# A decoder block in one launch: F0 from 10 to 8, two of w_down's sums in place, seven raw slots in the down projection

## The reference, cut to what matters

```python
x = x + concat([o_diff, o_nsa]) @ w_out            # 512 x 1024
h = rms_norm(x, norm2)
x = x + (silu(h @ w_gate) * (h @ w_up)) @ w_down   # w_gate, w_up 1024 x 2816, w_down 2816 x 1024
return rms_norm(x, final_norm)
```

## Time and profile before

| | us |
|---|---|
| median of 3 runs | 660.74 (659.76 to 660.91) |
| the profiled execution, its own time | 660.69 |
| its span, first to last instruction | 658.9 |
| PE busy in the span | 646.3 (98%) |
| DVE, ACT, POOL busy | 452.1, 348.5, 265.2 |
| plain stage from tile 1's up on | 329.99 to 425.66 |
| mixed stage | 425.66 to 545.87 |
| down stage, to the last matmul | 545.87 to about 652.4 |

### The profile page before, as it was taken

One profiled execution on the slowest core, in us unless ns is written; L12 is line 12 of the kernel. 1 busy time (PEld: TensorE's weight loads), 2 busy tenths in 40 slices (PEclk: granted clock), 3 DMA queues, 4 the chain that ended last, 5 costly groups with the idle time before them and its releaser, 6 DMA issues.

```text
span 658.9 us, 11055 instructions
## 1 busy us (share of the span) xinstructions
PE 646.3 (98%) x3915; PEld 570.2 (87%) x3915; DVE 452.1 (69%) x929; ACT 348.5 (53%) x689; POOL 265.2 (40%) x158
## 2 busy tenths in 40 slices
PE   8999999999999999999999999999999999999996
PEld 7988988888899887888877888899999998888884
DVE  5434437745655777634489987469888797788894
ACT  7546446778654568615332362344444445655663
POOL 4766343585242440224466767343443320000222
PEclk9999999999999999999999999999999999999999
DMA  8989969469894982144699999887677858766553
GB/s 247 268 179 243 284 187 216 112 193 367 228 267 113 246 168 65 45 159 118 160 298 300 289 282 283 209 253 213 188 225 208 256 176 274 261 189 201 183 171 127
DMA packets 114774, 139.22 MB, mean 211 GB/s; under 512 B 5044, under 2 KB 74784, under 8 KB 114720
## 3 DMA queue, kind: packets, MB, share of 16 engines
q1 hardware_dynamic: 97880, 107.35, 51.4%
q0 software_dynamic: 14176, 26.64, 22.6%
q10 hardware_dynamic: 2664, 4.53, 2.0%
HBM read 132.19 MB, written 54.81 MB: 284 GB/s over the span
## 4 chain that ended last, share of the span: by engine, by line
PE 81%; issue 8%; POOL 7%; DVE 2%; ACT 1%; DMA 1%; POOLq 0%; DVEq 0%; ACTq 0%
PE bank L776 8%; PE bank L778 8%; PE bank L777 8%; PE bank L795 7%; PE bank L797 7%; PE bank L796 7%; PE bank L1107 6%; PE bank L1105 6%; PE bank L1106 6%; PE bank L948 6%; POOL w_lo L728 4%; PE bank L924 3%; PE bank L908 2%; PE bank L909 2%; POOL down_sums L746 1%
## 5 line engine op out<-in xcount | busy, mean ns | idle before, releaser
L728 POOL TENSOR_TENSOR w_lo<-raw,w_hi 128x1024 fp32r<-128x1024 f32 (+1 forms) x76 | 191.1, 2518 | 261.9 <-ACT w_hi L1148 261.2
L1148 ACT CAST w_hi<-raw 128x1024 fp32r<-128x1024 f32 (+1 forms) x141 | 144.3, 1028 | 151.6 <-PE bank L1107 43.8
L795 PE MATMUL bank<-xT_hi,w_hi 128*128 128x512 f32 x272 | 108.8, 400 | 1.7 <-POOL w_lo L728 1.4
L797 PE MATMUL bank<-xT_hi,w_lo 128*128 128x512 f32 x272 | 107.0, 393 | 0.0
L796 PE MATMUL bank<-xT_lo,w_hi 128*128 128x512 f32 x272 | 106.8, 393 | 0.0
L1774 DVE TENSOR_TENSOR w_lo<-raw,w_hi 128x1024 fp32r<-128x1024 f32 x66 | 79.4, 1204 | 33.3 <-ACT w_hi L1148 33.3
L1617 DVE CUSTOM_DVE_ANT_0 bank<-bank,bias 128x128 f32<-128x128 f32 (+3 forms) x96 | 47.6, 497 | 78.0 <-PE bank L909 42.1
L795 PEld LDWEIGHTS bank<-xT_hi,w_hi 128*128 128x128 f32 x272 | 51.2, 188 | 13.1 <-POOL w_lo L728 1.7
L797 PEld LDWEIGHTS bank<-xT_hi,w_lo 128*128 128x128 f32 x272 | 51.1, 188 | 11.7
L796 PEld LDWEIGHTS bank<-xT_lo,w_hi 128*128 128x128 f32 x272 | 51.3, 188 | 9.9 <-issue 0.2
L1229 ACT ACTIVATE E<-bank,nmax 128x128 f32<-128x128 f32 (+3 forms) x80 | 42.5, 532 | 32.5 <-DVE nmax L1617 31.6
(11 more groups left out here) (280 smaller groups left out, 1609.3 us busy)
## 6 DMA issues: line engine op xcount, KB each, us to landing
raw<-mixed_sums SPq DMA_DIRECT2D x24, 512.0 KB, 4.6
raw<-in_w_gate_dram SPq DMA_DIRECT2D x22, 512.0 KB, 6.5
raw<-in_w_in_dram SPq DMA_DIRECT2D x20, 512.0 KB, 5.9
down_sums<-in_w_down_dram SPq DMA_DIRECT2D x20, 512.0 KB, 10.4
raw<-down_sums SPq DMA_DIRECT2D x20, 512.0 KB, 4.3
raw<-in_w_up_dram SPq DMA_DIRECT2D x16, 512.0 KB, 5.3
raw<-in_w_down_dram SPq DMA_DIRECT2D x15, 512.0 KB, 3.5
mixed_sums<-in_w_up_dram SPq DMA_DIRECT2D x12, 512.0 KB, 12.1
```

The source lines that it names most:

```text
L728: nc.gpsimd.tensor_tensor(wv_lo(k)[:, 0:n], raw[:, k % RAW_SLOTS, 0:n], wv_hi(k)[:, 0:n].bitcast(F32), ALU.subtract).then_inc(s_split, 1)
L795: nc.tensor.matmul(bank[:, :], hi, xT_hi[:, kt, :], start=kt == 0, stop=False)
L797: return nc.tensor.matmul(bank[:, :], lo, xT_hi[:, kt, :], start=False, stop=kt == KT - 1)
L1148: nc.scalar.copy(wv_hi(k)[:, 0:n], raw[:, k % RAW_SLOTS, 0:n]).then_inc(s_whi, 1)
```

## The change

F0 becomes 8, so tiles 8 and 9 are a seventh mixed pair. `mixed_sums` covers 14 tiles and takes 28 sums: for the last two tiles one block of two tiles and four steps. The order of RING is turned so that the first unit takes a bank of gate tiles. The plain stage has 16 chunks; SP makes copies beside 12 of them (every fourth has none) and four in the mixed stage, 40 in all.

In the down stage the products come in another order: A11, S3 (T3), S1 (T1), S2 (T2), A12, S4, A22 (T4). `down_sums` has two places instead of four. T3 and T1 are copied and added as before. T2 = T3 + a quarter is made by adding the quarter into T3's place, group by group, once S3's load of that group has landed in SBUF; T4 in T2's place in the same way after S2's loads. So POOL's loop runs to the last chunk, 12 copies go, and 52 accumulating DMAs are issued instead of 48. Only product 3 is in RUNNING, and it goes to three quarters of the output.

Down chunks use seven raw slots: the three of before and four of `raw_more`, which lies where `xa` (the left halves of units 0 and 1) was, so SP waits for unit 1 of the last pair before it loads there. The order in which quarters of x come back (`BACK`) and in which the output is normed (`NORMED`) follows the new order of products.

The core of the diff:

```diff
@@ -113,20 +114,21 @@
-PRODUCTS = [(A11, ("w", 0, 0), 0), (S1, ("sum", T1), 1), (S2, ("sum", T2), 0), (A12, ("w", 1, 0), 2),
-            (S3, ("sum", T3), 0), (S4, ("w", 1, 1), 1), (A22, ("sum", T4), 0)]
+PRODUCTS = [(A11, ("w", 0, 0), 0), (S3, ("sum", T3), 1), (S1, ("sum", T1), 0), (S2, ("sum", T2), 2),
+            (A12, ("w", 1, 0), 0), (S4, ("w", 1, 1), 1), (A22, ("sum", T4), 0)]
-RUNNING = (2, 4)
-QUARTERS = [[(0, 0, 1)], [(1, 1, 1), (0, 1, 1)], [(0, 1, -1)], [(0, 0, 1)], [(1, 1, -1), (1, 0, 1)], [(0, 1, 1)], [(1, 0, 1)]]
+RUNNING = (3,)
+QUARTERS = [[(0, 0, 1)], [(1, 1, -1), (1, 0, 1)], [(1, 1, 1), (0, 1, 1)], [(0, 1, -1), (1, 1, -1), (1, 0, 1)], [(0, 0, 1)],
+            [(0, 1, 1)], [(1, 0, 1)]]
-F0 = 10
+F0 = 8
 SUMS = [(T3, (0, 1), ("w", 1, 1)), (T1, (0, 1), ("w", 0, 0)), (T2, (0, 0), ("sum", T3)), (T4, (1, 0), ("sum", T2))]
-WIDE = 4
-
-BACK = {(0, 5): (0, 0), (1, 1): (0, 1), (1, 3): (1, 1), (2, 1): (1, 0)}
+OF_DOWN = [(T3, (0, 1), ("w", 1, 1)), (T1, (0, 1), ("w", 0, 0)), (T2, T3, ("w", 0, 0)), (T4, T2, ("w", 1, 0))]
+PLACE = {T3: 0, T2: 0, T4: 0, T1: 1}
+
+BLOCKS = [(0, 4, 0, 2), (0, 4, 2, 2), (4, 4, 0, 2), (4, 4, 2, 2), (8, 4, 0, 2), (8, 4, 2, 2), (12, 2, 0, 4)]
+
+BACK = {(0, 5): (0, 0), (1, 1): (1, 1), (1, 3): (1, 0), (2, 1): (0, 1)}
-    for wides in ((0, 1), (2,)):
+    for blocks in ((0, 1, 2, 3), (4, 5, 6)):
         for to, begin, add in SUMS:
-            todo += [("mixed", to, (w_, kp), begin, add) for w_ in wides for kp in range(2)]
-    for to, begin, add in SUMS:
+            todo += [("mixed", to, (b,), begin, add) for b in blocks]
+    for to, begin, add in OF_DOWN:
         todo += [("down", to, (g,), begin, add) for g in range(GROUPS_M)]
     return todo
+    mixed0, down_from = n_fill + 2 * F0, n_fill + 2 * F0 + N_UNIT * N_PAIR
     copy_at = [6 + i for i in range(10)] + [27 + i // 2 for i in range(14)]
-    copy_at += [n_fill + i for i in range(20)] + [n_fill + 2 * F0 + 4 + 10 * i for i in range(4)]
-    add_at = copy_at[0:16] + [31] * 8 + copy_at[24:]
+    copy_at += [n_fill + i for i in range(16) if i % 4 != 3] + [mixed0 + 4 + 10 * i for i in range(4)]
+    in_place = [down_from + GROUPS_M + 3 + i for i in range(6)] + [down_from + 3 * GROUPS_M + 3 + 2 * i for i in range(6)]
+    add_at = copy_at[0:16] + [31] * 8 + copy_at[24:] + in_place
+    assert len(add_at) == len(todo)
+        with ExitStack() as more_raw:
+
+            raw_more = sb("raw_more", [P, MORE_SLOTS, 1024], F32, more_raw)
-        RING = [ps[0], ps[6], ps[3], ps[4], ps[5], ps[2], ps[7], ps[1]]
+        RING = [ps[6], ps[3], ps[4], ps[5], ps[2], ps[0], ps[7], ps[1]]
...
-        NORMED = [(0, 0), (1, 0), (2, 1), (3, 1), (0, 1), (1, 1), (2, 0), (3, 0)]
+        NORMED = [(2, 1), (3, 1), (0, 0), (1, 0), (0, 1), (1, 1), (2, 0), (3, 0)]
...
-                return sums[what[1], m0:m1, :, :].rearrange("k p n -> p k n")
+                return sums[PLACE[what[1]], m0:m1, :, :].rearrange("k p n -> p k n")
...
+        def slot_of(k):
+
+            d = (k - down0) % (RAW_SLOTS + MORE_SLOTS)
+            return d if k >= down0 and d >= RAW_SLOTS else ((down0 + d) if k >= down0 else k) % RAW_SLOTS
+
+        def raw_at(k):
+            n = slot_of(k)
+            return raw_more[:, n - RAW_SLOTS, :] if n >= RAW_SLOTS else raw[:, n, :]
...
-                if k >= RAW_SLOTS:
-                    low_done(sp, k - RAW_SLOTS)
-                dst = raw[:, k % RAW_SLOTS, :]
-                signal = s_raw[k % RAW_SLOTS]
+                held = [m for m in range(k) if slot_of(m) == slot_of(k)]
+                if held:
+                    low_done(sp, held[-1])
+                elif slot_of(k) >= RAW_SLOTS:
+                    sp.wait_ge(s_chunk, late(("mixed", (N_PAIR - 1, 1))))
+                dst = raw_at(k)
+                signal = s_raw[slot_of(k)]
...
-                kind, to, at_, _, add = todo[i]
-                pool.wait_ge(s_copied[i % 4], 16 * (i // 4 + 1))
+                kind, to, at_, begin, add = todo[i]
+                if i < len(copy_at):
+                    pool.wait_ge(s_copied[i % 4], 16 * (i // 4 + 1))
+                else:
+                    raw_landed(pool, index[("down", ([x_[1] for x_ in PRODUCTS].index(("sum", begin)), at_[0]))])
...
-            for k in range(down0):
+            for k in range(len(chunks)):
```

More of the change, by code:

```diff
@@ L53 @@
 RAW_SLOTS = 3
+MORE_SLOTS = 4
 SPLIT_SLOTS = 4
@@ L444, in hymba_block @@
         s_final_g = sem("s_final_g")
-        s_raw = [sem(f"s_raw{i}") for i in range(RAW_SLOTS)]
+        s_raw = [sem(f"s_raw{i}") for i in range(RAW_SLOTS + MORE_SLOTS)]
         s_bias = [sem(f"s_bias{i}") for i in range(BIAS_SLOTS)]
@@ L516, in hymba_block @@
         run = up_n
-        sums = nc.dram_tensor("down_sums", (len(SUMS), FP, P, 512), F32).ap()
+        sums = nc.dram_tensor("down_sums", (2, FP, P, 512), F32).ap()
         down0 = index[("down", (0, 0))]
-        NORMED = [(0, 0), (1, 0), (2, 1), (3, 1), (0, 1), (1, 1), (2, 0), (3, 0)]
+        NORMED = [(2, 1), (3, 1), (0, 0), (1, 0), (0, 1), (1, 1), (2, 0), (3, 0)]
         adds = [(n, rows_, dh, u) for n in range(N_PROD) for rows_, dh, _ in QUARTERS[n] for u in range(2)]
@@ L568, in sum_part @@
                 return part(what, at_[0])
-            return mixed_part(what, F0 + WIDE * at_[0], WIDE, 2 * at_[1], 2)
+            f0, n, k0, n_k = BLOCKS[at_[0]]
+            return mixed_part(what, F0 + f0, n, k0, n_k)
         def sum_done(eng, kind, to, at_):
@@ L663, in _ @@
                     if UNITS[j][1][0] == "sum":
-                        for kp in range(2):
-                            sum_done(sp, "mixed", UNITS[j][1][1], (2 * p_ // WIDE, kp))
+                        for b, (f0, n, _, _) in enumerate(BLOCKS):
+                            if f0 <= 2 * p_ < f0 + n:
+                                sum_done(sp, "mixed", UNITS[j][1][1], (b,))
                     sp.dma_start(dst[:, 0:1024].rearrange("p (k n) -> p k n", k=4),
@@ L673, in _ @@
                     sp.dma_start(dst[:, 0:chunk_cols(k)].rearrange("p (k n) -> p k n", k=src.shape[1]), src).then_inc(signal, 16)
-                for i in [i for i in range(len(todo)) if copy_at[i] == k]:
+                for i in [i for i in range(len(copy_at)) if copy_at[i] == k]:
                     _, to, _, begin, _ = todo[i]
@@ L708, in raw_landed @@
         def raw_landed(eng, k):
-            loads = sum(2 if chunks[m][0] == "vg" else 1 for m in range(k % RAW_SLOTS, k + 1, RAW_SLOTS))
-            eng.wait_ge(s_raw[k % RAW_SLOTS], 16 * loads)
+            loads = sum(2 if chunks[m][0] == "vg" else 1 for m in range(k + 1) if slot_of(m) == slot_of(k))
+            eng.wait_ge(s_raw[slot_of(k)], 16 * loads)
         @block.gpsimd
@@ L727, in split @@
                 high_done(pool, k)
-                nc.gpsimd.tensor_tensor(wv_lo(k)[:, 0:n], raw[:, k % RAW_SLOTS, 0:n],
+                nc.gpsimd.tensor_tensor(wv_lo(k)[:, 0:n], raw_at(k)[:, 0:n],
                                         wv_hi(k)[:, 0:n].bitcast(F32), ALU.subtract).then_inc(s_split, 1)
@@ L1147, in weights_hi @@
                     act.wait_ge(s_chunk, late(chunks[was]))
-                nc.scalar.copy(wv_hi(k)[:, 0:n], raw[:, k % RAW_SLOTS, 0:n]).then_inc(s_whi, 1)
+                nc.scalar.copy(wv_hi(k)[:, 0:n], raw_at(k)[:, 0:n]).then_inc(s_whi, 1)
             def square(src, junk, col, n):
@@ L1773, in split_down @@
                 n = chunk_cols(k)
-                nc.vector.tensor_tensor(wv_lo(k)[:, 0:n], raw[:, k % RAW_SLOTS, 0:n],
+                nc.vector.tensor_tensor(wv_lo(k)[:, 0:n], raw_at(k)[:, 0:n],
                                         wv_hi(k)[:, 0:n].bitcast(F32), ALU.subtract).then_inc(s_dlo, 1)
```

## The result

The changed kernel takes **664.25 us** (median of 7 runs, 662.76 to 666.16) where the kernel before takes 660.81 in the same job; ratio 1.0054, 95% interval 1.0036 to 1.0072. That is 3.4 us slower; 658.2 was forecast, and the range ended at 660.8.

What follows compares the result with a forecast made beforehand. PE, busy 646.3 of 658.9 us, was taken to bound the kernel. The terms gave 660.69 - 2.07 - 1.39 + 0.90 = 658.13 us, from the median 658.2, with a range of 656.8 to 660.8.

Steps and rivals of the forecast that it cites:

- Part 1: Tiles 8 and 9 become a mixed pair: PE time falls from 22.10 to 20.04 us, 2.07 us saved.
- Part 2: Plain stage: fewer copies let loads land earlier, so PE's two w_lo pauses go; 1.39 us saved, bounds 0 and 1.39.
- Part 3: Crossing to the mixed stage, two tiles earlier: DVE's backlog makes unit 4's w_lo late; 0.9 us lost, bounds 0 and 2.4.
- DVE's list: Crossing: DVE's work from 399.42 through unit 4's split, 12.15 us, ending at 411.6 with 2.0 us to spare.
- the 5.65: Crossing: us for up 7 and the seven short operations behind it, taken from the old kernel, already holding one POOL collision.
- Part 4: RING's order, the seventh pair's sums and the moved copies: no cost, hidden by PE.
- Part 5: Down stage: same 462 matmuls, 106.53 us; the new slots, DVE's longer run and the sums in place cost zero.
- Seven raw slots only load earlier: Down stage: the added raw slots bring loads forward and cost nothing, as ACT and DVE already keep up.
- The rival of sums one after another: Down stage: accumulations wait for each other, 8.6 us each; PE stands 8.4 us, 666.6 us; chance 0.05.
- The eight additions: Down stage, product 3's turn on DVE: eight where the longest run was six, 1.24 us more, still 1.5 us early; no cost.
- The sum: Whole kernel: 660.69 - 2.07 - 1.39 + 0.90 = 658.13 us, from the median 658.2.

Runs made afterwards that it cites:

- before_early_81: Kernel before, with two of chunk 31's eight additions put behind POOL's subtraction of chunk 32, and that held until 81 exps are done; 660.49 us, ratio 1.0013.
- split_83: Changed kernel, with POOL waiting before its subtraction of chunk 32 until ACT has done 83 exps; 663.11 us, ratio 1.0043.
- no_adds: Changed kernel without the twelve accumulations of T2 and T4 (products take T3's sums instead), and SP not waiting for them; 658.83 us, ratio 0.9977.
- three_slots: Changed kernel with only the three earlier raw slots in the down stage (MORE_SLOTS 0 instead of 4); 676.16 us, ratio 1.0244.
- back_late: Changed kernel with SP's four loads of x moved behind later chunks, the first from (0, 5) to (1, 3); 658.96 us, ratio 0.9981.
- sp_stands: Changed kernel with the four x loads behind later chunks, but SP still waiting at chunk (0, 5) until the last mixed unit ends; 661.60 us, ratio 1.0015.

## Why the prediction was wrong

**Part 1** right: 22.10 to 20.04 us, 2.06. The estimate from the Trainium skill (TensorE: Matmul & The Clock Gate, Back-to-back issue gap), 2.37, was 0.3 too high.

**Part 2** right: 1.4 us taken, 1.4 measured. Both pauses are gone. POOL's fourth and fifth subtractions of the stage, the two that PE had waited for, in the kernel after:

```profile
346.31 2.82 POOL L754 TENSOR_TENSOR w_lo<-raw,w_hi 128x1024 fp32r<-128x1024 f32 x1
349.70 2.40 POOL L754 TENSOR_TENSOR w_lo<-raw,w_hi 128x1024 fp32r<-128x1024 f32 x1 [0.58 <-ACT w_hi L1177]
```

They end at 349.13 and 352.10; before they ended at 353.14 and 359.24, just ahead of the starts in the earlier trace rows. Two things changed at once in the kernel after, the copies and the start of the stage. In before_early_81, with every copy in its place, the subtractions end at 352.96 and 358.37, and a start 0.59 us later is enough to lose both pauses. But split_83, where the stage starts at 329.90, no later than before, has no pause either: its two subtractions end at 348.36 and 351.85. So the earlier loads are enough by themselves. Taking the copies alone out of the kernel before wasn't tried.

**Part 3** mis-sized: 0.9 taken, 0 measured. The mixed stage is seven times 20.04. Of DVE's list, the two products took 2.9 us where about 0.8 was put (a collision), and the seven short operations hold one collision, as the 5.65 had it: so the list has the one extra collision that was to make unit 4 0.2 us late. But it begins 2.5 us earlier than I put it (first line, against 399.42 in the earlier trace rows), and unit 4's split (second line) ends at 411.45, 2.8 us before PE wants it at 402.80 + 4 x 2.862 = 414.25.

```profile
396.92 0.68 DVE L1885 TENSOR_TENSOR gate_n<-bank,sq 128x512 f32<-128x512 f32 x1
...
410.23 1.22 DVE L1803 TENSOR_TENSOR w_lo<-raw,w_hi 128x1024 fp32r<-128x1024 f32 x1
```

**Part 4, "Nothing", failed**: a change in when a batch of accumulations ends moved the subtraction behind it on POOL's queue. I had asked what a moved copy does to PE, not what is queued behind it on POOL. It costs 0.6 to 0.8 us, shown in the traces from both sides (0.76 back in split_83, 0.59 lost in before_early_81), and between 0.3 and 1.7 in the other runs. The Trainium skill (SBUF — State Buffer, Who interferes with whom) has the exclusive lock that fits it; I used it for 128x512 additions and not for a 128x8 product. In these traces the time was set by POOL's instruction and not by the size of DVE's. In no_adds and three_slots the product is recorded 0.44 and 0.24 us ahead of the subtraction and still ends with it, after 3.31 and 3.11 us; which of the two was really first can't be read from these traces.

**Part 5, "Zero" and "Seven raw slots only load earlier", is the step that failed**, 4.8 of the 5.5 us lost. The rival of sums one after another had the right stage and the wrong mechanism: the first pause is at 569.43, product 1, not at 3 or 6 where a load waits for its sum. Two errors make it up.
- I took the landing from the rows' median over a quiet stage, 4.6 us, for a stage to which I added accumulations. The row of the loaded stage had 11.7. And the engines' time says that they would be full: twelve accumulations (ten of 512 and two of 256 KB) at 2.86 us for 512 KB are 31 us in the stage's first 55. Of these 55 the loads already took some 39 us in the kernel before (a share of 0.84, 0.74, 0.62 and 0.63 in four stretches of 15 us): 70 us do not go into 55. That shows that loads will be late, not that PE waits: back_late has the same transfers, and there the loads begin early enough.
- "Seven raw slots only load earlier" is not so: I didn't read SP's order against the new schedule. The load of x that waits for the last mixed unit was there before too, but SP came to it when it was free. With seven slots SP comes to it 6 us early and stands, so product 1's first load is issued 0.66 us behind the stage's start and not 5.88 ahead of it, as in back_late. Each alone is free (no_adds, back_late); together they cost 4.8 us.

The eight additions were fine: in no_adds and back_late DVE has the same eight and PE doesn't pause. The fourth pause after, 0.4 us with the slower start behind it, ahead of 618.37, ends with the split behind them (618.32), but counted from the stage's start less the three pauses DVE begins that run 64.9 us in, 1.2 us later than in back_late (63.7): its loads had been late.

**The sum** with measured terms: 660.7 - 2.06 - 1.4 + 0 + 0.67 + 4.8 = 662.7, the profiled 662.76. The median lies 1.5 us above this execution; for that no cause is shown beyond what split_83's trace suggests (a longer pause in the down stage, and the slower clock behind it).

## What to carry to other kernels

Cost an added DMA by the time that it takes the DMA engines, and take the landing of its neighbours from a stage that is already so loaded. When a queue gets more to do, look in its order for instructions that wait: a stand that costs nothing while the DMA engines have time to spare (no_adds) is paid when they are full, and more slots can bring the queue to it early. And a batch that ends earlier moves all that is queued behind it, perhaps onto an instruction of another engine.

## What the runs showed of the hardware

- By their queues' shares, an accumulating DMA of 512 KB from DRAM to DRAM took 2.86 us of all 16 engines (in both kernels), a load of that size 1.49.
- With a DMA share of 1.07 to 1.09, loads of 512 KB landed in 9.9 to 14.1 us; without the accumulations (no_adds, 543 to 603 us, share 0.76) in 5.1 and 6.7.
- A DVE product of 128x8 took 2.58 us in place of 0.23, and ended with GpSimd's subtraction (236.08 and 236.05).
- TensorE's granted clock differs between runs in the same place. From 248 to 252 us PE is busy 2.96 or 2.97 us in the kernels before, after, back_late and sp_stands; in the next 4 us it has 1.00 in the first two, 0.66 and 0.63 in the others, and sp_stands stays at 0.52 (about 1.2 GHz) until 260. From the exp at 249.08 to the one at 258.53 it is 9.45 us in the kernel before and 9.44 between the same two after; in back_late it is 10.58 and in sp_stands 12.29. Why isn't known; none of it is in the sum above.
- After a pause in the plain and down stages the matmul lasted 0.50 in place of 0.39 us, and the next start was 0.10 to 0.11 us later than it would be.
